# Hybrid decoder trunk on one core: the sums of the gate weight blocks done by GpSimd instead of VectorE

## What is computed

```python
h = rmsnorm(x, g_mix)
proj = h @ w_in
za, zb, zc, zg = jnp.split(proj, IN_SPLITS, axis=-1)
...
gates = jax.nn.sigmoid(zg.reshape(nb, s, N_BRANCH, D_MODEL) + b_gate)
merged = gates[:, :, 0] * ya + gates[:, :, 1] * yb + gates[:, :, 2] * yc
return x + merged @ w_o
```

## Time and profile before

| what | value |
|---|---|
| median of 3 runs | 900.63 us (900.39 to 900.72) |
| the profiled execution | 900.4 us, its span 898.7 us |
| granted TensorE clock | 0.999 |
| PE busy | 888.4 us, 5292 matmuls |
| DVE busy | 596.2 us, 711 instructions |
| ACT busy | 385.7 us, 555 instructions |
| POOL busy | 57.5 us, 59 instructions |
| the gate stage | 192.8 to 382 us of the span |

### The profile page before, as it was taken

One profiled execution on the slowest core, in us unless ns is written; L12 is line 12 of the kernel. 1 busy time (PEld: TensorE's weight loads), 2 busy tenths in 40 slices (PEclk: granted clock), 3 DMA queues, 4 the chain that ended last, 5 costly groups with the idle time before them and its releaser, 6 DMA issues.

```text
span 898.7 us, 13165 instructions
## 1 busy us (share of the span) xinstructions
PE 888.4 (99%) x5292; PEld 793.1 (88%) x5292; DVE 596.2 (66%) x711; ACT 385.7 (43%) x555; POOL 57.5 (6%) x59
## 2 busy tenths in 40 slices
PE   9999999999999999999999999999999999999997
PEld 7998888889999998988888888899999999888886
DVE  5685666789577678755466476998888887433333
ACT  5654432345444444523244332554555445322223
POOL 0111000000000000024100053000000000000000
PEclk9999999999999999999999999999999999999999
DMA  9946332213322222672211122222322233322212
GB/s 350 364 168 265 110 105 94 94 47 99 137 93 95 94 100 89 226 289 94 92 49 51 44 94 107 81 95 97 127 103 93 93 116 117 117 93 94 94 48 94
DMA packets 16091, 108.17 MB, mean 120 GB/s; under 512 B 1840, under 2 KB 1968, under 8 KB 4016
## 3 DMA queue, kind: packets, MB, share of 16 engines
q1 hardware_dynamic: 13408, 93.99, 28.3%
q10 hardware_dynamic: 2176, 12.00, 3.5%
q0 software_dynamic: 464, 1.57, 0.5%
HBM read 101.26 MB, written 6.29 MB: 120 GB/s over the span
## 4 chain that ended last, share of the span: by engine, by line
PE 84%; DVE 10%; ACT 4%; issue 2%; DMA 1%; SPq 0%; POOLq 0%; POOL 0%; ACTq 0%; DVEq 0%
PE psum L1445 28%; PE psum L1447 27%; PE psum L1446 27%; DVE blk L870 2%; ACT blk L395 1%; DVE sig L1155 1%; DMA pack<-first 1%; DVE tl L870 1%; DVE wl L870 1%; DVE raw L1061 1%; DVE raw L1059 1%; DVE raw L1060 1%; DVE merged L1158 0%; ACT wh L395 0%; PE psum L1697 0%
## 5 line engine op out<-in xcount | busy, mean ns | idle before, releaser
L1445 PE MATMUL psum<-th,w7h 128*128 128x256 f32 x504 | 142.7, 283 | 0.3 <-ACT snap L395 0.3
L1447 PE MATMUL psum<-th,w7l 128*128 128x256 f32 x504 | 142.6, 283 | 0.0
L1446 PE MATMUL psum<-tl,w7h 128*128 128x256 f32 x504 | 142.6, 283 | 0.0
L870 DVE TENSOR_TENSOR wl<-raw,wh 128x2048 fp32r<-128x2048 f32 (+1 forms) x44 | 89.4, 2043 | 50.0 <-ACT wh L395 49.9
L1445 PEld LDWEIGHTS psum<-th,w7h 128*128 128x128 f32 x504 | 96.8, 192 | 0.6 <-issue 0.5
L1446 PEld LDWEIGHTS psum<-tl,w7h 128*128 128x128 f32 x504 | 96.8, 192 | 0.0
L1447 PEld LDWEIGHTS psum<-th,w7l 128*128 128x128 f32 x504 | 96.8, 192 | 0.0
L395 ACT ACTIVATE wh<-raw 128x2048 fp32r<-128x2048 f32 (+1 forms) x44 | 73.1, 1675 | 20.8 <-PE psum L1447 19.5
L1445 PE MATMUL psum<-hh,wh 128*128 128x512 f32 x192 | 75.0, 391 | 0.0
L1447 PE MATMUL psum<-hh,wl 128*128 128x512 f32 x192 | 74.7, 389 | 0.0
L1446 PE MATMUL psum<-hl,wh 128*128 128x512 f32 x192 | 74.7, 389 | 0.0
(11 more groups left out here) (265 smaller groups left out, 2197.3 us busy)
## 6 DMA issues: line engine op xcount, KB each, us to landing
raw<-weights SPq DMA_DIRECT2D x79, 1024.0 KB, 4.8
pack<-first SPq DMA_DIRECT2D x3, 768.0 KB, 7.9
vraw<-weights SPq DMA_DIRECT2D x2, 1024.0 KB, 12.1
xt<-xt SPq DMA_DIRECT2D x1, 2048.0 KB, 18.7
X<-x SPq DMA_DIRECT2D x2, 1024.0 KB, 27.7
X<-x ACTq DMA_DIRECT2D x1, 2048.0 KB, 10.1
memt<-memt SPq DMA_DIRECT2D x1, 1024.0 KB, 22.6
kv_store<-kh ACTq DMA_DIRECT2D x1, 1024.0 KB, 3.9
```

Of the source, the lines that this page charges most:

```text
L870: return V.tensor_tensor(dst, v, f32(hi), ALU.subtract)
L1445: nc.tensor.matmul(dst, lh, rh, start=start, stop=False, **kw)
L1446: nc.tensor.matmul(dst, lh, rl, start=False, stop=False, **kw)
L1447: return nc.tensor.matmul(dst, ll, rh, start=False, stop=stop, **kw)
```

## The change

The four sums of each gate panel move from DVE (`gate_prep`) to POOL, as a loop over the 12 panels, in place and in the same order. POOL waits for `lo_a`. DVE's `gate_prep_lo` gets a wait for `s2_ready`. In DVE's order for h = 1 to 5, the merge of tile 1 moves ahead of `gate_prep_lo` of the first panel, and the unsummed low parts of the second panel move ahead of the merge of tile 3. On ACT, keep u3 of the first panel moves ahead of the two pairs of the second panel.

```diff
--- before.py
+++ after.py
@@ -363,6 +363,16 @@
             pool.wait_ge(mixed, 4)
             pool.dma_start(wgr[:], wg_in).then_inc(wg_here, 16)
 
+            gp = nc.gpsimd
+            for i in range(NG):
+                w = raw[:, (GA0 + 3 * (i // 2) + i % 2) % SLOTS, :].rearrange("p (b f) -> p b f", b=4)
+                pool.wait_ge(lo_a, i + 1)
+                chain(gp.tensor_tensor(w[:, 2], w[:, 2], w[:, 0], ALU.subtract))
+                chain(gp.tensor_tensor(w[:, 0], w[:, 0], w[:, 1], ALU.subtract))
+                gp.tensor_tensor(w[:, 1], w[:, 1], w[:, 2], ALU.add).then_inc(s2_ready, 1)
+                pool.wait_ge(s2_ready, i + 1)
+                gp.tensor_tensor(w[:, 3], w[:, 3], w[:, 1], ALU.subtract).then_inc(s4_ready, 1)
+
             def sum_squares(ready, done):
 
                 for k in range(KT):
@@ -635,9 +645,9 @@
                 keep(first[1], 0, "s1")
                 keep(first[1], 0, "s5")
                 keep(first[1], 0, "u2")
+                keep(first[1], 0, "u3")
                 gate_pair_hi(*second, 0)
                 gate_pair_hi(*second, 1)
-                keep(first[1], 0, "u3")
 
                 keep(second[1], 1, "s1")
                 split_hi(second[0] + 1)
@@ -1044,27 +1054,19 @@
             for g in range(BT):
                 dve.wait_ge(acth_ready, g + 1)
                 lo(actl[:, g, :], bank[4 + g][:], acth[:, g, :]).then_inc(actl_ready, 1)
-            def raw_flat(s):
-                return raw[:, s, :].rearrange("p (b f) -> p b f", b=4)
-
             def raw_blocks(s):
                 return raw[:, s, :].rearrange("p (b k f) -> p b k f", b=4, k=4)
 
             def gate_prep(n, i):
 
-                w, blocks, p = raw_flat(n % SLOTS), raw_blocks(n % SLOTS), n % 2
+                blocks, p = raw_blocks(n % SLOTS), n % 2
                 dve.wait_ge(hi_a, i + 1)
                 lo(gate_lo[p][0], blocks[:, 1:4], gate_hi[p][0]).then_inc(lo_a, 1)
-                dve.wait_ge(lo_a, i + 1)
-                chain(V.tensor_tensor(w[:, 2], w[:, 2], w[:, 0], ALU.subtract))
-                chain(V.tensor_tensor(w[:, 0], w[:, 0], w[:, 1], ALU.subtract))
-                V.tensor_tensor(w[:, 1], w[:, 1], w[:, 2], ALU.add).then_inc(s2_ready, 1)
-                dve.wait_ge(s2_ready, i + 1)
-                V.tensor_tensor(w[:, 3], w[:, 3], w[:, 1], ALU.subtract).then_inc(s4_ready, 1)
 
             def gate_prep_lo(n, i):
                 blocks, p = raw_blocks(n % SLOTS), n % 2
                 dve.wait_ge(hi_s13, i + 1)
+                dve.wait_ge(s2_ready, i + 1)
                 lo(gate_lo[p][1], blocks[:, 0:2], gate_hi[p][1]).then_inc(lo_s13, 1)
                 dve.wait_ge(s4_ready, i + 1)
                 dve.wait_ge(hi_ready, n + 1)
@@ -1163,12 +1165,11 @@
                 gate_add(n - 2, i - 1, 1)
                 gate_prep(n, i)
                 merge(h - 1, 0)
+                merge(h - 1, 1)
                 gate_prep_lo(n, i)
-                merge(h - 1, 1)
-
                 merge(h - 1, 2)
+                gate_prep(n + 1, i + 1)
                 merge(h - 1, 3)
-                gate_prep(n + 1, i + 1)
                 gate_prep_lo(n + 1, i + 1)
 
                 gate_add(n, i, 0)
```

## The result

The changed kernel takes 906.44 us (median of 4 runs, 906.22 to 906.67) against 900.61 us before: a ratio of 1.0065 (95% interval 1.0048 to 1.0083), 5.8 us more. The forecast was 902.9 us, with a range up to 905.2. Its profiled execution has a span of 904.5 us, against 898.7.

A forecast was written before the change was run, and what follows sets the result against it. PE was taken as the bound (busy 888.4 of 898.7 us), so only its lateness counts. Terms -2.4 + 2.5 + 1.4 + 1.0 = +2.5 us on 900.4 gave 902.9 us; own range 901.0 to 905.2, whole range down to 898.9.

The forecast's parts named there:

- the pooling window: Ahead of the gate stage, DVE's window additions alternate with POOL's sums, so the last copy and PE come later: +1.0 us.
- products 3 and 4 of the second panel at h = 0 and h = 3 to 5: PE stops there for s1 and s5, kept after a later `gate_sum`: +1.4 us at h = 0, +2.5 us at h = 3 to 5.
- the price of a sum: Each gate-panel sum on POOL was taken as 1.15 us, blocked or not, from an addition that ended behind a DVE instruction.
- The multiplication of a tile by itself: POOL's residual-stage multiplication of the same 128x512 size, 1.04 us, taken as the low end for a sum.
- Keep u3: ACT keeps u3 before the second panel's pairs, so PE's stop at product 7 goes at h = 3, 4, 5: -2.4 us.
- The order of locks at merge 1: At h = 3, first panel, merge 1's addition on DVE is issued ahead of POOL's third sum, which then waits.
- DVE's order: The merges moved in DVE's queue at h = 1 to 5 were said to cost nothing in themselves.
- No lock: Rival, 17%: DVE and POOL do not hold each other at the window and the merges' additions; 898.9 us, not slower.
- Short sums: Rival, 22%: a POOL sum alone takes 1.04 us, h = 3 to 5 have no stop; 900.0 us.
- 1.62 us by itself: Rival, 6%: a POOL sum takes 1.62 us unblocked, both pairs come late and PE stops at product 2 too; 912 us.
- a wait for `lo_s13`: PE waiting for this low part was the sign given for long sums, which would show the forecast wrong.
- The estimate of 1.12 us: A POOL sum as a quarter of 4497 ns for 2048 elements; the change's total would be some 0.6 us less.

## Why the prediction was wrong in its size

The direction and the places were right. PE lost time where the text put it: in the pooling window, at products 3 and 4 of the second panel at h = 0 and h = 3 to 5, through `gate_sum` queued behind late low parts. It also lost time where the text had none, at product 4 for h = 1 and 2 and at product 2 for h = 0. The size was 2.3 times too small.

**The step that failed** is the price of a sum: "I take 1.15 us for a sum, blocked or not". A sum alone takes 1.295 us. The 1.15 us were read behind a hold, from the end of DVE's instruction on. An instruction that waits for the other engine seems to have its start-up behind it by then (this reading fits the times; no run looks inside). I had written that down for DVE (0.14 us less than alone) and not applied it to POOL. 1.15 + 0.14 = 1.29 could have been had from the earlier trace rows. Behind a hold a sum still ends after 1.15 us, so that half of the price was right. The multiplication of a tile by itself, 1.04 us, led further off: it is not the price of two different inputs. The forecast's own range ended at 1.25 us a sum, and the whole range at 905.2.

**What the 0.145 us did.** Four chained sums alone delay `gate_sum` by some 0.6 us. At h = 1 the forecast had 7.87 us from the low parts to `gate_sum`, with 0.45 to spare; in the profile after it is 8.52, and PE stops (0.64 us for h = 1 and 2). At h = 0 product 2 stops as well, 0.41 us late, for the low part in `hh`. At h = 3 the low parts end 4.34 us after the first panel's start instead of 4.24, and `gate_sum` comes 8.86 us after them instead of 8.34. Product 4 is late by 0.53 us, as forecast (0.54); product 3 by 0.77 instead of 0.08. So the stops are 1.5 us each instead of 0.84. The runs with shorter sums show that the length of a sum is what these stops hang on. They shorten the held sums too, so they do not part the price alone from the price behind a hold; and with sums near 1.15 us h = 3 cost less than the forecast's 0.84.

**The other terms.** Keep u3: -2.4 summed, -2.1 to -2.3 measured. Window: +1.0 summed, +1.0 measured. The order of locks at merge 1 came as reckoned: at h = 3 the merge's addition was issued at 285.58, the third sum at 285.81, and the sum waited. DVE's order was rightly priced at nothing for itself, but its worth beside slow sums, 7 us, was not stated.

**The rivals.** None came. "No lock" falls with the window additions of 1.67 us and with the run that left the merge's product in PSUM. "Short sums" needed 1.04 us. "1.62 us by itself" falls with the 1.29 us seen alone, and its 912 us were too much. Yet the sign that I gave for it, a wait for `lo_s13`, came once, at h = 0, with 1.29 us. The truth lay between the forecast and that rival, where I had no case: 1.29 us.

The Trainium skill ("SBUF — State Buffer", "Who interferes with whom") has the lock as the runs show it; it also says that a DVE instruction with at most one SBUF input does not contend, which the additions of 0.69 us with one input in PSUM bear out. The estimate of 1.12 us that I made from the Trainium skill ("GPSIMD Engine Reference", section 3.1) is contradicted by the 1.295 us here. The times for 512 and 448 columns give 2.1 ns a column and, as an estimate, some 0.2 us that do not depend on the width; a quarter of a duration at 2048 columns leaves out most of these.

## What to carry to other kernels

A duration read behind a wait is too short for an instruction alone (1.15 against 1.295 us here); before it is used for an instruction that runs alone, add what the same trace shows others save. Where the path has slack of a few tenths of a microsecond and an instruction is chained four times, its price must be known to a few hundredths (0.07 us less of a sum was worth 2.3 us, the next 0.07 us 3.3), and the range must cover that difference. Moving work to an idle engine gains nothing when another engine is the bound: here the whole gain was one kept result moved ahead of two copies, and the slower sums ate it until the kept sum was also moved ahead in DVE's queue.

## What the runs showed that was not expected

Long stops of PE cost more than their length in some runs. With keep u3 late PE stops for 2.76 us at h = 3, 4 and 5. PE's waits, the timeline after the stop at h = 3, and the stretches behind the stops (PEclk is the last but two of the columns, of full speed):

```profile
PE psum L1446 <- ACT gsnap L405: 12.7, 7, 2.8
...
304.63 0.58 PE L1446 MATMUL psum<-gth,blk 128*128 128x256 f32 x1 [2.76 <-ACT gsnap L405]
...
305.22 0.41 PE L1448 MATMUL psum<-gth,blk 128*128 128x256 f32 x1
...
305.44 0.41 PE L1446 MATMUL psum<-gth,blk 128*128 128x256 f32 x1
...
304.60:308.00 3.40, 3.37 (x16) 3.38 (x17) 2.04 (x3) 0.00 (x0) 0.00 (x0) 0.50 0.25 67
...
308.00:312.00 4.00, 4.00 (x25) 4.00 (x25) 0.29 (x1) 1.85 (x2) 0.00 (x0) 0.67 0.49 205
...
312.00:318.00 6.00, 6.00 (x52) 6.00 (x51) 2.67 (x2) 2.53 (x6) 0.00 (x0) 1.00 0.35 115
...
341.00:345.00 4.00, 3.68 (x18) 3.68 (x19) 2.53 (x3) 0.27 (x1) 0.00 (x0) 0.57 0.33 86
...
376.80:380.00 3.20, 3.11 (x26) 3.11 (x27) 2.41 (x3) 0.04 (x1) 0.00 (x0) 1.00 0.30 51
```

Before the stop the matmuls start 0.12 us apart; after it 0.21 to 0.22. From 304.60 to 308 the granted clock is 0.50, which is the lower level, 1.2 GHz; from 308 to 312 it is 0.67 on average, then 1.00 again. After the stop that ends at 341.32 the clock is low too (0.57 up to 345), but not after the one of the same length that ends at 376.89. The five runs took 914.04 to 920.01 us with mean clocks of 0.999 to 0.992, the fastest at 0.999, so the lower clock fits the slower runs; only the one of 917.87 us has a trace. The stops of 1.65 us in this run and of 1.6 us in the one with the old DVE order left the clock at 1.00. What decides between the two outcomes after 2.76 us was not tried.
